# Sixteen gate units of the mixer moved from the merge phase into the attention stream

## The reference, cut to what matters

```
for l in range(DEPTH):
    x = x + 0.5 * swiglu_ffn(x, ...)
    h = rms_norm(x, mix_norm[l])
    x = x + hybrid_mixer(h, ...)
    x = x + 0.5 * swiglu_ffn(x, ...)

hybrid_mixer:
    o_a, o_b, o_c = stick_breaking(...), nsa(...), dsa(...)      # widths 256, 512, 256
    g_a, g_b, g_c = split(sigmoid(h @ w_gate), 3)                # w_gate: 1024 x 3072
    merged = g_a * (o_a @ w_br_a) + g_b * (o_b @ w_br_b) + g_c * (o_c @ w_br_c)
    return merged @ w_out
```

## Time and profile before

| | |
|---|---|
| median of three runs | 3850.59 us (3847.55 to 3850.78) |
| profiled execution | 3848.09 us, of which its span 3846.5 us |
| busy of the span: PE, DVE, ACT, POOL | 96%, 51%, 39%, 4% |
| mean granted clock of TensorE | 0.954 |
| attention slots, layer 0 and layer 1 | 563.70 to 801.30, 1932.26 to 2152.90 us |
| merge phase with output, layer 0 | 804.76 to 1031.89 us |

### The profile page before, as it was taken

How to read it: one execution, slowest core, us unless ns; L and a number is a source line. 1 busy time by engine, 2 the same in 40 slices (tenths; PEclk the granted TensorE clock), 3 DMA queues, 4 the chain that set the end, 5 groups by cost and what they waited for, 6 DMA issues and landing times.

```text
span 3846.5 us, 48674 instructions
## 1 busy us (share of the span) xinstructions
PE 3700.8 (96%) x17516; PEld 2947.8 (77%) x17516; DVE 1947.0 (51%) x3253; ACT 1498.0 (39%) x2201; POOL 141.4 (4%) x133
## 2 busy tenths in 40 slices
PE   8999979999999999999889999999999998999998
PEld 6888866578888888888755688888887876878886
DVE  4443465754544344433658544443388764334433
ACT  4432244553343334422456543433233334334431
POOL 0000000000100000000000001000000001010001
PEclk9999986899999999999979999999999987989999
DMA  3223330022232222233210122223322211212231
GB/s 131 97 94 109 102 118 1 1 72 98 84 102 98 99 98 95 96 104 112 94 42 1 61 103 82 102 98 102 113 93 84 70 42 33 100 65 88 98 101 68
DMA packets 89165, 322.37 MB, mean 84 GB/s; under 512 B 10639, under 2 KB 10895, under 8 KB 89032
## 3 DMA queue, kind: packets, MB, share of 16 engines
q1 hardware_dynamic: 84384, 304.35, 23.4%
q0 software_dynamic: 3840, 13.17, 1.0%
q10 hardware_dynamic: 808, 3.07, 0.2%
HBM read 318.40 MB, written 10.02 MB: 85 GB/s over the span
## 4 chain that ended last, share of the span: by engine, by line
PE 59%; PEld 25%; issue 8%; DVE 5%; ACT 3%; PEldq 1%; POOLq 0%; DMA 0%; POOL 0%; DVEq 0%; ACTq 0%
PE bank L253 15%; PE bank L255 15%; PE bank L254 15%; PEld bank L255 8%; PEld bank L253 8%; PEld bank L254 8%; PE bank L1379 2%; PE bank L1406 2%; PE bank L847 1%; PE bank L867 1%; PE bank L838 1%; PE bank L1395 1%; DVE val L1533 1%; PE bank L877 1%; PE bank L948 1%
## 5 line engine op out<-in xcount | busy, mean ns | idle before, releaser
L249 DVE TENSOR_TENSOR unit_lo<-unit_raw,unit_hi 128x1024 fp32r<-128x1024 f32 x572 | 700.8, 1227 | 826.4 <-ACT unit_hi L244 817.7
L253 PE MATMUL bank<-h_hi,unit_hi 128*128 128x512 f32 x2688 | 1065.4, 396 | 21.8 <-DVE unit_lo L249 13.1
L254 PE MATMUL bank<-h_lo,unit_hi 128*128 128x512 f32 x2688 | 1056.8, 393 | 0.0
L255 PE MATMUL bank<-h_hi,unit_lo 128*128 128x512 f32 x2688 | 1056.2, 393 | 0.0
L244 ACT ACTIVATE unit_hi<-unit_raw 128x1024 fp32r<-128x1024 f32 x572 | 600.9, 1052 | 388.2 <-PE bank L255 375.4
L253 PEld LDWEIGHTS bank<-h_hi,unit_hi 128*128 128x128 f32 x2688 | 511.1, 190 | 133.3 <-DVE unit_lo L249 14.5
L255 PEld LDWEIGHTS bank<-h_hi,unit_lo 128*128 128x128 f32 x2688 | 511.0, 190 | 108.6
L254 PEld LDWEIGHTS bank<-h_lo,unit_hi 128*128 128x128 f32 x2688 | 511.2, 190 | 107.0 <-issue 1.7
L253 PE MATMUL bank<-act_hi,unit_hi 128*128 128x512 f32 x880 | 346.7, 394 | 0.0
L255 PE MATMUL bank<-act_hi,unit_lo 128*128 128x512 f32 x880 | 345.0, 392 | 0.0
L254 PE MATMUL bank<-act_lo,unit_hi 128*128 128x512 f32 x880 | 341.5, 388 | 0.0
(11 more groups left out here) (275 smaller groups left out, 4359.4 us busy)
## 6 DMA issues: line engine op xcount, KB each, us to landing
unit_raw<-in_units SPq DMA_DIRECT2D x572, 512.0 KB, 3.3
bias_rows<-bias_once POOLq DMA_DIRECT2D x2, 3840.0 KB, 16.7
bias_t<-bias_rows POOLq DMA_DIRECT2D x16, 256.0 KB, 3.1
x<-in_x SPq DMA_DIRECT2D x4, 512.0 KB, 7.8
out_x<-x SPq DMA_DIRECT2D x8, 256.0 KB, 2.1
mixer_gains<-in_mixer_gains ACTq DMA_DIRECT2D x2, 736.0 KB, 5.0
mixer_constants<-in_mixer_constants ACTq DMA_DIRECT2D x2, 560.0 KB, 3.8
bias_t<-bias_rows POOLq DMA_DIRECT2D x8, 128.0 KB, 2.6
```

The lines of the kernel that those rows point to most:

```text
L249: nc.vector.tensor_tensor(w_lo[u % SLOTS][:], raw[u % SLOTS][:], w_hi[u % SLOTS][:].bitcast(F32), ALU.subtract).then_inc(unit_lo, 1)
L253: nc.tensor.matmul(out_ap, w_h, r_h, start=first, stop=False)
L254: nc.tensor.matmul(out_ap, w_h, r_l, start=False, stop=False)
L255: return nc.tensor.matmul(out_ap, w_l, r_h, start=False, stop=last)
```

## The change

Units of gates a and b (16 a layer) now stand in the list right behind the first phase, a and b of tile 0, then of tile 1, and so on; the merge phase has 16 units, c gates and branches, in the order c0 c1 c2 b0 c3 b1 ... c7 b5 b6 b7.

- The gate unit 0 is multiplied in three parts in the tail of the first phase (12, 6 and 6 matmuls). Part of the tail's chain moves ahead by some units: the compressed keys' product to after unit 29, and the gates' sigmoid and the keys' root on ScalarE into the loop.
- In the attention gate units use bank 7 and unit slots 0 and 1 alone. 12 matmuls of unit 1 stand ahead of slot 0, then a table gives the number of matmuls for each slot (132, 102, 74 and 59 by block), between that slot's scores and its values. The 19 last of them are of unit 16, which is c gate 0; its last five run ahead of the fence.
- ScalarE copies each finished gate out of bank 7 unscaled, GpSimd sends it to memory, and the next eviction waits for that to land. ScalarE splits the unit after next one slot after a unit's last, VectorE two slots after it.
- `qk_hi` now lies in the place of x; x is stored at the start of the first phase and loaded again at the start of the merge phase. The outputs of attention groups have bank 5 alone; the values that open a group go behind the transposes. Some steps of the compressed and stick-breaking attention move by a slot.
- In the merge phase gates a and b of a tile come back from memory in one transfer of 512 KB, VectorE scales them by the norm, ScalarE takes one sigmoid over 1024 columns. Branch and c products have two sets of banks. The loop over m is written out.

```diff
...
+GATE_UNITS, GATE_SLOTS = 16, 2
...
+    idle = Place(nc, w_idle_at)
+    qk_hi = nc.alloc_sbuf_tensor_at("qk_hi", [P, KD * S], F32R, offset=x_at)
+    dk_hi = idle.tensor("dk_hi", S, F32R)
...
+    sig_ab = [part3.tensor(f"sig_ab{i}", 2 * S) for i in range(2)]
+    sig_c = [part3.tensor(f"sig_c{i}", S) for i in range(3)]
...
+    x_kept = nc.dram_tensor("x_kept", (P, KD * S), F32, kind="Internal").ap()
+    gates_kept = nc.dram_tensor("gates_kept", (GATE_UNITS, P, S), F32, kind="Internal").ap()
...
+    def gate_products(pe, r, e, first, end):
+
+        if first == 0:
+            pe.wait_ge(unit_lo, SLOTS * r + e + 1)
+        if first == 0 and e > 1:
+            pe.wait_ge(s["gate_z"], e - 1)
+        w_h, w_l = w_hi[e % GATE_SLOTS], w_lo[e % GATE_SLOTS]
+        for i in range(first, end):
+            k = slice(i // 3 * P, (i // 3 + 1) * P)
+            w, h = ((w_h, h_hi), (w_h, h_lo), (w_l, h_hi))[i % 3]
+            mm = nc.tensor.matmul(bank[7][:], w[:, k], tile(h, i // 3), start=(i == 0), stop=(i == 23), skip_group_check=True)
+        if end == 24:
+            mm.then_inc(unit_used, 1)
...
+                if kv == 1:
+                    gate_products(pe, r + 8, 0, 0, 12)
                 pe.wait_ge(s["hid_n"], 2 * kv + 2)
...
+        gate_products(pe, r + 8, 0, 12, 18)
         pe.wait_ge(s["hid"], 4)
...
         mm.then_inc(s["cmp_mm"], 1)
+        gate_products(pe, r + 8, 0, 18, 24)
         pe.wait_ge(s["roped"], 13)
...
         ends = {13: 0, 17: 1, 21: 2}
...
+        act.wait_ge(unit_used, SLOTS * (r + 8) + 2)
+        nc.scalar.activation(gate_z[:], bank[7][:], ACT.Copy)
         act.wait_ge(s["cmp_turned"], 1)
         nc.scalar.activation(kc_t[:], bank[5][:, 0:NC], ACT.Copy)
+        act.wait_ge(s["x_sent"], 16)
...
-        return bank[(5, 7)[group_no(b, k) % 2]]
-
+    GATE_FILL = ((8, 4, 8, 6, 10, 10, 12, 2, 12, 10, 2, 0, 8, 4, 9, 3, 9, 7, 8, 0),
+                 (8, 10, 4, 2, 10, 10, 4, 8, 8, 8, 5, 0, 4, 3, 6, 1, 4, 1, 6, 0),
+                 (4, 9, 2, 2, 1, 9, 9, 6, 8, 6, 5, 0, 4, 0, 1, 0, 2, 0, 6, 0),
+                 (3, 5, 1, 0, 5, 2, 9, 5, 5, 5, 0, 0, 1, 0, 5, 2, 5, 5, 1, 0))
...
+    def gate_split_at(q, late):
+
+        return next((e for e in range(2, GATE_UNITS + 2) if q == gate_end[e - 2] + 1 + late), None)
...
+    def gate_hi(act, r, e):
+
+        act.wait_ge(raw_full[e % SLOTS], 16 * (r + e // SLOTS + 1))
+        act.wait_ge(unit_used, SLOTS * r + e)
+        nc.scalar.activation(w_hi[e % GATE_SLOTS][:], raw[e % SLOTS][:], ACT.Copy).then_inc(unit_hi, 1)
+
+    def gate_lo(dve, r, e):
+
+        dve.wait_ge(unit_hi, SLOTS * r + e + 1)
+        nc.vector.tensor_tensor(w_lo[e % GATE_SLOTS][:], raw[e % SLOTS][:], w_hi[e % GATE_SLOTS][:].bitcast(F32),
+                                ALU.subtract).then_inc(unit_lo, 1)
+
+    def gate_copy(act, r, e, sent):
+
+        act.wait_ge(unit_used, SLOTS * r + e + 2)
+        act.wait_ge(gate_sent, sent + 16 * e)
+        nc.scalar.activation(gate_z[:], bank[7][:], ACT.Copy).then_inc(s["gate_z"], 1)
+
...
-            if kb == 0 and bt in (0, 2, 4) and g >= 2:
-                pe.wait_ge(s["o_out"], g - 1)
+            if kb == 0 and bt in (0, 2, 4) and g >= 1:
+                pe.wait_ge(s["o_out"], g)
...
+        gate_products(pe, r, 1, 0, GATE_FIRST)
         for q in range(SLOT_END + 1):
             b, at = divmod(q, JOBS)
             if q < SLOTS2:
                 scores(q)
-            if tile_of(q - LAG):
+            if gate_piece(q):
+                gate_products(pe, r, *gate_piece(q))
+            if tile_of(q - LAG) and not opens_group(q):
                 values(*tile_of(q - LAG))
             if tile_of(q):
                 turn(*tile_of(q))
+            if opens_group(q):
+                values(*tile_of(q - LAG))
             for bh in index_heads(q):
...
+            if gate_ended(q):
+                gate_copy(act, r, gate_ended(q), 16 * GATE_UNITS * l)
...
+            if gate_split_at(q, 0):
+                gate_hi(act, r, gate_split_at(q, 0))
...
+        pool.dma_start(gates_kept[0], gate_z[:]).then_inc(gate_sent, 16)
         bias_copies_pool(pool, l)
-        for b in range(TB):
-            for k in range(2):
+        for q in range(SLOT_END + 1):
+            if gate_ended(q):
+                pool.wait_ge(s["gate_z"], gate_ended(q))
+                pool.dma_start(gates_kept[gate_ended(q)], gate_z[:]).then_inc(gate_sent, 16)
+            if merged(q) and merged(q)[1] < 2:
+                b, k = merged(q)
                 g = 2 * b + k
...
             if q < SLOTS2:
                 reduce(q)
+            if gate_split_at(q, 1):
+                gate_lo(dve, r, gate_split_at(q, 1))
...
+    def c_unit(m):
+
+        return m if m < 2 else 2 * m - 2
+
+    def br_unit(m):
+        return 2 * m + 3 if m < KD - 2 else MERGE_UNITS - KD + m
+
+    def branch_bank(m, br):
+        return bank[((3, 4, 5), (1, 2, 6))[m % 2][br]]
+
+    def c_bank(m):
+        return bank[(7, 0)[m % 2]]
...
     def mix3_pe(pe, f, r):
+        gate_products(pe, r - GATE_UNITS // SLOTS, GATE_UNITS, GATE_LAST, 24)
         fence(pe, f)
-        with pe.Fori(0, KD) as m:
-            for g in range(3):
-                pe.wait_ge(s["gate_free"], 3 * m + g + 1)
-                unit_product(pe, r + m, g, bank[g][:], h_hi, h_lo)
-            pe.wait_ge(s["branches"], m + 1)
-            pe.wait_ge(s["o_lo"], KD)
-            pe.wait_ge(unit_lo, SLOTS * (r + m) + 3 + 1)
+        for u in range(1, MERGE_UNITS):
+            kind, m = MERGE_ORDER[u]
+            if kind == "c":
+                if m >= 2:
+                    pe.wait_ge(s["gate"], m - 1)
+                unit_product(pe, r, u, c_bank(m)[:], h_hi, h_lo)
+                continue
+            if m == 0:
+                pe.wait_ge(s["o_lo"], KD)
+            if m >= 2:
+                pe.wait_ge(s["branches"], m - 1)
+            pe.wait_ge(unit_lo, SLOTS * r + u + 1)
             for k in range(KD):
                 br = 0 if k < 2 else 1 if k < 6 else 2
                 w = slice(k * P, (k + 1) * P)
-                mm = three(bank[3 + br][:], w_hi[3][:, w], w_lo[3][:, w], tile(o_hi, k), tile(o_lo, k), k in (0, 2, 6), k in (1, 5, 7))
+                mm = three(branch_bank(m, br)[:], w_hi[u % SLOTS][:, w], w_lo[u % SLOTS][:, w], tile(o_hi, k), tile(o_lo, k),
+                           k in (0, 2, 6), k in (1, 5, 7))
             mm.then_inc(unit_used, 1)
         pe.wait_ge(s["m_lo"], KD - 1)
-        rd = r + KD
+        rd = r + MERGE_UNITS // SLOTS
...
+        def gates_in(m):
+            act.dma_start(sig_ab[m % 2][:].rearrange("p (e t) -> p e t", e=2),
+                          gates_kept[2 * m:2 * m + 2].rearrange("e p t -> p e t")).then_inc(s[f"sig_in{m % 2}"], 16)
+
...
+        act.wait_ge(gate_sent, 16 * GATE_UNITS * l + 16 * GATE_UNITS)
+        gates_in(0)
+        gates_in(1)
+        act.dma_start(x[:], x_kept).then_inc(s["x_back"], 16)
         for t in range(KD):
             nc.scalar.activation(tile(o_hi, t), tile(o_t, t), ACT.Copy).then_inc(s["o_hi"], 1)
-        with act.Fori(0, KD) as m:
...
+        def scale_ab(m):
+            dve.wait_ge(s[f"sig_in{m % 2}"], 16 * (m // 2 + 1))
+            ab = sig_ab[m % 2][:].rearrange("p (e t) -> p e t", e=2)
+            nc.vector.tensor_tensor(ab, ab, rs_full[:].unsqueeze(1).to_broadcast([P, 2, S]), ALU.mult).then_inc(s["ab_scaled"], 1)
+
...
+            dve.wait_ge(s["sig"], m + 1)
+            dve.wait_ge(s["sig_ab"], m + 1)
+            nc.vector.tensor_tensor(part[0][:], sig_ab[m % 2][:, 0:S], branch_bank(m, 0)[:], ALU.mult)
+            nc.vector.tensor_tensor(part[1][:], sig_ab[m % 2][:, S:2 * S], branch_bank(m, 1)[:], ALU.mult)
+            nc.vector.tensor_tensor(sig_c[m % 3][:], sig_c[m % 3][:], branch_bank(m, 2)[:], ALU.mult).then_inc(s["branches"], 1)
+            dve.wait_ge(s["branches"], m + 1)
             nc.vector.tensor_tensor(part[0][:], part[0][:], part[1][:], ALU.add).then_inc(s["part_sum"], 1)
             dve.wait_ge(s["part_sum"], m + 1)
-            nc.vector.tensor_tensor(val[0][:], part[0][:], part[2][:], ALU.add).then_inc(s["m_val"], 1)
+            nc.vector.tensor_tensor(val[0][:], part[0][:], sig_c[m % 3][:], ALU.add).then_inc(s["m_val"], 1)
             dve.wait_ge(s["m_hi"], m + 1)
-            a = bass.ds(m * S, S)
-            nc.vector.tensor_tensor(m_lo[:, a], val[0][:], m_hi[:, a].bitcast(F32), ALU.subtract).then_inc(s["m_lo"], 1)
...
+            if m + 1 < KD:
+                scale_ab(m + 1)
+        dve.wait_ge(s["x_back"], 16)
...
```

More of the change, by code:

```diff
@@ L543, in mix1_pe @@
                 mm.then_inc(s["hid_tr"], 1)
-        pe.wait_ge(s["t_out"], 3 * TB)
+            if u == 29:
+                pe.wait_ge(s["hid"], 2)
+                for g in range(G):
+                    mm = nc.tensor.matmul(bank[2][0:NC, g * HD:(g + 1) * HD], hid[g][:, 0:NC], w2(0), start=True, stop=True)
+                mm.then_inc(s["cmp_keys"], 1)
+        gate_products(pe, r + 8, 0, 12, 18)
```

(36 more changed lines are left out.)

172 lines of the change are left out of this document (94 added, 78 removed).

## The result

The changed kernel took 3805.2 us (median of four runs, 3797.8 to 3819.5) against 3850.7 us (four runs, 3847.6 to 3863.1): a ratio of 0.9889, 95% interval 0.9861 to 0.9916. The forecast was 3737 with a range from 3705, so the sign was right, and the drop was 45.5 us where 113 were forecast. The profiled execution took 3798.9 us; by the forecast's own sum it would have taken 3848.1 - 113.4 = 3734.7. These 64 us are to be found.

The account below looks back on a forecast made before the run. TensorE was taken to bound the kernel nearly everywhere. Layer 0 at -65.2 us and layer 1 at -48.2 (merge phase -93.6 each, attention grown to 266) gave -113.4: 3848.1 - 113.4 + 2.5 = 3737 us, range 3705 to 3789.

Parts of the forecast that it names:

- What bounds the kernel: Whole kernel: TensorE's nearly everywhere, busy 96% of the span; something is left only in the two attention phases.
- The clock restored, both layers alike: Attention: slots of both layers take the same time, 250 to 290 us, with the clock over 0.95.
- The rival in which it stays down: Attention: clock stays low in 46% and 30% of slots, growth 107.6 and 94.2 us; 3865 us, chance 0.06.
- in name only: Attention: moved matmuls wait for their split weights, so work moves only in name; about 3850 us, chance 0.02.
- the row at 0.51: Kernel before, 20 us from 601: PE recorded busy 19.87 us, clock 0.51; taken as evidence for the clock staying down.
- I take 278 - 14.5 + 2 = 266: Attention per layer: 278 us with nothing hidden, less 14.5 idle filled, plus 2 for the single output bank.
- the matmuls at 0.228: Attention: 367 added matmuls at 0.228 us each, the merge phase's price, 83.6 us per layer.
- Rival "nothing hidden", 3831: Attention: the chain sets each slot, pieces come on top, no clock gain; -20 us in all, chance 0.06.
- Merge phase, -93.6: Merge phase per layer: -92.8 for 17 units gone, -2.4 earlier start, +0.3 before the fence, +1.3 at the end.
- The late end: End of merge phase: two branches in a row make PE wait some 1.3 us more, between 0 and 5.
- First mixer phase, 0: Tail of the first mixer phase: added gate matmuls change its time by 0, between -3 and +3 us.
- Moved data, 0: x stored to memory and loaded back, 2 MB each way, plus unit loads: cost 0, at most 2 us.

Follow-up runs that it names:

- e4: Changed kernel with splits and evictions of the attention's gate units cut to 8 columns; attention 0.9 us shorter in layer 0, 0.6 in layer 1.
- e2: Changed kernel with 11 of the 24 matmuls of gate units 1 to 15 left out; attentions 24.3 and 17.0 us shorter.
- e3: Changed kernel with only the first and last matmul of gate units 1 to 15 kept; attentions 271 and 268.5 us, clock 0.75 and 0.76.
- e6: Changed kernel with the same 367 gate matmuls per attention in 31 pieces in place of 66; attentions 289.6 and 288.5 us.
- e7: Changed kernel, c0's bank scaled right behind unit 2's split, bias rows copied at slot 70; merge phases 139.1 us, attention 6 us longer (layer 0), 2.5 shorter (layer 1).
- e9: Kernel before with only the change's single output bank for the values; first phases 180.8 us, attentions 5.6 and 0 us above 195 + 0.39 per lower-clock us.
- e1: Changed kernel run again unedited on another chip; 3817.7 us beside 3874.8 for the kernel before there.
- e11: Changed kernel unedited, timed six times beside the kernel before on one chip; 49.3 us between their medians, profiled attentions 286.1 and 285.9 us.

## Why the prediction was wrong, step by step

- **What bounds the kernel**: right. TensorE sets the attention too: e4 took 32 us of VectorE and ScalarE work away and got 2.4 at most; e2 took matmuls away and got 31 of their 36.5 us, less what the clock took.
- **The clock restored, both layers alike**: right. From 110 and 65 us at the lower clock it went to 10 in each. At 0.39 us each that is (99 + 55) x 0.39 = 60 us, more than the whole drop of the profiled execution (49 us). By this sum the clock is the change's gain. The rival in which it stays down is out, and so is "in name only": the matmuls left the merge phase. The forecast had set the row at 0.51 against the rule of the Trainium skill (TensorE: Matmul & The Clock Gate, What's actually happening) that the array's own activity releases the clock: the granted clock of 0.98 with the fill and 0.75 without it (e3) agrees with the rule.
- **"I take 278 - 14.5 + 2 = 266"**: this is the step that failed, by 16.5 us a layer. Its 278 at full clock with nothing hidden was met, 282.6 less 0.45 x 10.2 us of lower clock being 278.0, but by terms that cancel: it held neither seams nor a new wait, and some idle time was filled. Three terms ate what was to be hidden. First, the lower clock that stays, 4.6 us. Second, the matmuls at 0.228. They stand between matmuls of another shape, and I had priced them from a stretch of nothing but their own. A fit over 1,414 slots at full clock of the ten profiled executions with the change's stream (a constant for each slot number, one price a matmul, one a piece) gives 0.223 and 0.11 us: 367 x 0.223 + 66 x 0.11 = 89 us, 5.5 above the 83.6. This is an estimate and not a sharp one: fitted to the smallest sum of absolute misses in place of squares, the same slots give 0.228 and 0.19, some 13 above. As e6 shows, the seam price wasn't had back by fewer pieces. Third, the wait for gate_z, 3.3 us, which the forecast had at 0: it looked at what GpSimd's queue does at the merges, and not at the copy ahead of the stream, and so named as the longest waits others than the one that came. e7 took 2.5 us of it away in layer 1. What remains, 16.5 - 4.6 - 5.5 - 3.3 = 3 us (by the second fit -4), is idle time that was less, or more, hidden than taken: 7.2 us of it is still recorded, of which 3.3 is that wait. So the wait is measured, the lower clock's part is worked out from the low us that are, and how the rest divides between seams and idle time stays open.
- **Rival "nothing hidden", 3831**: in this sense half right. Nothing net was hidden, but it had also written off the clock's gain; its two halves should have been priced apart.
- **Merge phase, -93.6**: 7.5 off. The matmuls went as counted. The forecast checked that VectorE fits a pair of units in the steady state, and "put it at nothing"; at the start VectorE has all eight o_lo and a split ahead of the first gate's bank, and PE stood 4.5 to 4.9 us, after which the clock fell. e7 gave back 7.2 with one instruction moved. The late end, taken at 1.3 us, came to 2.8: from start to start the two waits hold 1.66 and 2.04 us, less two matmuls of 0.23 and the 0.4 waited before.
- **First mixer phase, 0**: right for the change, yet it cost 13.8 us in the profiled execution. e9 shows the same in code that the change doesn't touch. The forecast summed one execution in which neither layer had it, and gave no room in the range to what the kernel before does by itself from one execution to the next.
- **Moved data, 0**: nothing in the waits speaks against it; no run tested it by itself.

In all: 33.5 (attention) + 15 (merge) + 13.8 (first phase) + 2 = 64 us.

## What to carry to other kernels

Where TensorE is recorded busy and yet the clock is low, large matmuls put into the stream can be paid for in part by the clock, even if they hide behind nothing: 73 us of them cost 12 to 14 here. Price them at their seams, and take none of the recorded idle time as free. And when work moves across a queue, write down what stands in each engine's queue at the first use, not in the steady state: both waits that were found (the bias rows ahead of the first store, eight o_lo ahead of the first gate) are of the start.

## What the runs showed of the hardware that was not expected

The clock's low stretches come and go between executions of the same instructions. The kernel before has an attention of 220.3 or 237.2 us with the same instructions, in either layer. The first mixer phase takes 169 us, or 179 to 183. The two stretches below lie 131 to 155 us into that phase of the kernel after, in layer 0 and in layer 1, at a granted clock of 1.00 and 0.50. The phases execute the same instructions in the same order. PE gets through 410 matmuls in the one and 148 in the other, but 308 of the 410 are short ones (L559), most of which the slow layer reaches later; the 146 that start in the slow stretch take 13.5 us in layer 0, against 23.9.

```profile
528.10:552.00 23.90, 21.57 (x410) 20.52 (x411) 18.23 (x60) 15.56 (x27) 0.00 (x0) 1.00 0.42 139
1856.30:1880.20 23.90, 23.90 (x148) 23.57 (x149) 13.14 (x55) 5.83 (x13) 0.00 (x0) 0.50 0.15 45
```

In the 26 such phases of 13 profiles, 16 were long and 10 short. In 25 of them there is an earlier short stretch at the lower clock near the phase's start, and where it begins tells the two apart: 1.9 to 2.1 us after the phase's first matmul in all ten short ones, 1.1 to 1.8 or at 2.2 in fifteen long ones. So a shift of some tenths of an us, of the work against whatever sets the clock, goes with 10 to 13 us more a hundred us later. The bounds were drawn after the phases were sorted, and no experiment shifted the work on purpose, so that the shift is the cause is not shown. The Trainium skill (TensorE: Matmul & The Clock Gate, Part 1: The HAM clock gate) says that what watches the activity runs free of the kernel's start, so that the same kernel differs from run to run; the starts agree: in layer 0 of the unchanged kernel after, one lies at 1.9 us in the first profile and at 1.6 in e1 and e11. It puts the loss of warming up at under 1% of a typical kernel's span; here the effect comes in the middle, and one such phase is 13.8 of 3800 us. Of the kernel before, and of e9 ahead of its stream, 2 of 6 were long, of the kernel after 5 of 6; whether the change makes them more frequent is left open by so few.
